# Earlier row splits, and one selection for the first two experts, in an encoder layer with a mixture of experts

## The reference

```python
h = (_layer_norm(x) * (1 + scale2) + shift2)                 # 512 rows of 1024
logit_g = h @ w_router_group + b                             # 4 groups, top 1
logit_e = h @ w_router_expert + b                            # 8 experts of that group, top 2
# each token goes to 2 of 32 experts, weighted with the softmax of its logits
y = (silu(xb @ w_exp_gate[e]) * (xb @ w_exp_up[e])) @ w_exp_down[e]
f = sum of the two weighted y of a token
x = LN(alpha * x + gate2 * f)
```

## Time and profile before

| | us |
|---|---|
| median of 3 runs | 959.95 |
| lowest, highest | 956.57, 960.58 |
| profiled execution | 959.74 |
| its span, first to last instruction | 958.10 |
| routing, first TensorE instruction behind the output projection | 430.74 |
| first product of expert 0 | 455.25 |

### The profile page before, as it was taken

The page is one execution under the profiler, slowest core; times in us unless marked ns, Lnnn a source line. Parts: engine busy times, 40 slices in busy tenths (PEclk is TensorE's granted clock), DMA queues, the critical chain, the costliest instruction groups (busy, mean ns, idle before and its releaser), DMA issues.

```text
span 958.1 us, 11740 instructions
## 1 busy us (share of the span) xinstructions
PE 908.5 (95%) x4381; PEld 547.7 (57%) x4381; DVE 375.9 (39%) x646; ACT 244.6 (26%) x357; POOL 113.6 (12%) x142
## 2 busy tenths in 40 slices
PE   3999999999999999999999999999998999998994
PEld 2567766888888888786454444444444444443331
DVE  4533443565344236798531232222221231322135
ACT  2422244432333225446411111101011110111024
POOL 2210366000001000000000000000000000000031
PEclk9999999999999999999999999999998999999997
DMA  9985654265565623809999999999999999999974
GB/s 370 348 282 175 253 218 177 89 230 208 200 240 147 183 91 114 278 0 401 384 404 400 410 427 425 427 424 429 429 426 424 375 395 427 426 426 427 423 290 136
DMA packets 47510, 295.53 MB, mean 308 GB/s; under 512 B 5046, under 2 KB 7190, under 8 KB 32082
## 3 DMA queue, kind: packets, MB, share of 16 engines
q1 hardware_dynamic: 37216, 263.99, 68.6%
q0 software_dynamic: 9616, 29.02, 9.0%
q10 hardware_dynamic: 610, 1.66, 0.5%
HBM read 275.81 MB, written 23.09 MB: 312 GB/s over the span
## 4 chain that ended last, share of the span: by engine, by line
PE 88%; DVE 3%; DMA 2%; issue 2%; SPq 2%; ACT 2%; POOL 0%; DVEq 0%; POOLq 0%; ACTq 0%
PE bank L627 85%; PE bank L929 2%; SPq L397 2%; DMA modraw<-in_w_mod 1%; DMA y_first<-round_y,pos_y 1%; PE bank L832 0%; PE bank L692 0%; DVE wo_lo L1766 0%; DMA round_y<-yout,store_row 0%; PE bank L911 0%; DVE y_second L2189 0%; DVE y_second L2202 0%; ACT w_hi L1181 0%; POOL y_second L615 0%; ACT sg_hid L1415 0%
## 5 line engine op out<-in xcount | busy, mean ns | idle before, releaser
L627 PE MATMUL bank<-down_w,hid_t 128*64 128x512 f32 x512 | 123.9, 627 | 8.1 <-issue 5.6
L627 PE MATMUL bank<-h_hi,w_hi 128*128 128x512 f32 x320 | 124.8, 390 | 0.3 <-ACT h_hi L1215 0.3
L627 PE MATMUL bank<-h_hi,w_lo 128*128 128x512 f32 x320 | 124.7, 390 | 0.0
L627 PE MATMUL bank<-h_lo,w_hi 128*128 128x512 f32 x320 | 124.6, 397 | 0.0
L627 PE MATMUL bank<-gate_w,x_by_pair 128*64 128x512 f32 x256 | 112.5, 592 | 0.8 <-ACT x_by_pair L1181 0.8
L627 PE MATMUL bank<-up_w,x_by_expert 128*64 128x512 f32 x256 | 112.6, 592 | 0.0
L627 PE MATMUL bank<-gate_w,x_by_expert 128*64 128x512 f32 x256 | 112.5, 592 | 0.0
L627 PE MATMUL bank<-up_w,x_by_pair 128*64 128x512 f32 x256 | 112.5, 592 | 0.0
L1415 ACT ACTIVATE sg_hid<-bank 64x512 f32<-64x512 f32 x33 | 19.5, 591 | 315.0 <-PE bank L627 315.0
L2047 DVE TENSOR_TENSOR sg_hid<-bank,sg_hid 64x512 f32<-64x512 f32 x32 | 22.2, 695 | 196.4 <-ACT sg_hid L1415 196.3
L1601 DVE TENSOR_TENSOR w_lo<-raw,w_hi 128x1024 fp32r<-128x1024 f32 x56 | 68.5, 1225 | 76.9 <-ACT w_hi L1181 76.8
(11 more groups left out here) (329 smaller groups left out, 1310.3 us busy)
## 6 DMA issues: line engine op xcount, KB each, us to landing
down_w<-in_w_exp_down SPq DMA_DIRECT2D x32, 2048.0 KB, 16.6
gate_w<-in_w_exp_gate SPq DMA_DIRECT2D x30, 2048.0 KB, 16.0
up_w<-in_w_exp_up SPq DMA_DIRECT2D x30, 2048.0 KB, 20.5
modraw<-in_w_mod SPq DMA_DIRECT2D x24, 1024.0 KB, 7.7
raw<-in_w_in SPq DMA_DIRECT2D x9, 2048.0 KB, 9.8
round_y<-zrow POOLq DMA_DIRECT2D x6, 2048.0 KB, 7.7
raw<-in_w_branch_b SPq DMA_DIRECT2D x2, 2048.0 KB, 9.5
raw<-in_w_branch_a SPq DMA_DIRECT2D x2, 2048.0 KB, 10.6
```

Of the source, the lines that this page charges most:

```text
L627: return pe.matmul(out, lhsT, rhs, start=start, stop=stop, skip_group_check=True)
```

## The change

- ScalarE makes the high parts during the routing: the first right behind the copy of tile 2, the other three behind the copy of tile 3.
- GpSimd, not VectorE, makes the low parts, each when its high part and the transposes of its tile are done.
- Experts 0 and 1 are selected together from the split rows: one `sel` operation on VectorE in place of two, 16 `float32r` products in place of 24 float32 ones. `selected_alone` goes.
- The columns of both experts are made in two halves of four chunks; `x_rows_b` is a second row buffer.
- `gate_up` of expert 1 runs right behind that of expert 0; the transposes of expert 0's hidden rows stand in its middle, and `down` of expert 0 comes after it. Expert 1 has a PSUM bank and a hidden buffer of its own (`sg_second`).
- The selection for experts 2 and 3 moves behind `down` of expert 0.
- SyncE loads expert 3's halves in four DMAs instead of eight, and issues expert 4's gate and up weights ahead of expert 2's down weights.
- ScalarE's scaling of `res` (128x4096) moves behind the first `Silu`.

```diff
+        x_rows_b = at("x_rows_b", [128, 512], f32, S0 + 3584)
...
+        sg_second = at("sg_second", [128, DE], f32, T0 + 34816)
...
-            for e in range(3, NEXP - 2):
...
+            done = sp.value_load(tab[0:1, 1, 1:2], min_val=0, max_val=16)
+            for half, freed, loaded in ((slice(0, KC // 2), gum_half, e_half), (slice(KC // 2, KC), m_sem["gum"], e_gu[0])):
+                sp.wait_ge(freed, 1)
+                sp.sem_inc(sp_go, 1)
+                sp.wait_ge(x_sem["gum"], done + 1)
+                sp.sem_inc(sp_go, 1)
+                for tile, w in ((gate_w[0], w_exp_gate), (up_w[0], w_exp_up)):
+                    sp.dma_start(tile[:, half, :], gate_src(w, 3)[:, half, :]).then_inc(loaded, 16)
+            next_gate_up(4, 1)
+            next_down(2, 0)
+            next_down(3, 1)
+            for e in range(5, NEXP - 2):
+                next_gate_up(e, e % 3)
                 next_down(e - 1, (e - 1) % 2)
...
+            for i in range(TILES):
+                pool.wait_ge(act_h2hi, i + 1)
+                pool.wait_ge(pe_rt, 2 * i + 2)
+                pool.tensor_tensor(h2_lo[i][:, :, :], h2[i][:, :, :], h2_hi[i][:, :, :].bitcast(f32), ALU.subtract).then_inc(pool_h2lo, 1)
...
-            def selected_alone(a, bank, chunks):
...
-            def selected(chosen, bank, c):
-
-                for i in range(TILES):
+            def selected(chosen, bank, c, tiles=range(TILES), parted_rows=None):
+                for i in tiles:
+                    if parted_rows is not None:
+                        pe.wait_ge(parted_rows, i + 1)
                     for piece in (h2_hi, h2_lo):
                         x = mm(bank[:, :], chosen[:, i, :, :].rearrange("p a s -> p (a s)"), piece[i][:, 4 * c:4 * c + 4, :].rearrange("p k n -> p (k n)"),
                                start=(i == 0 and piece is h2_hi), stop=(i == TILES - 1 and piece is h2_lo))
...
+            def first_columns(half):
+                pe.wait_ge(m_sem["xr"], half + 1)
+                x_transposes((x_rows, x_rows_b)[half], B[4 + half]).then_inc(m_sem["xtr"], 1)
...
+            def first_experts():
+                main_gate_up(0)
+                main_gate_up(1)
+                main_down(0)
+                pe.wait_ge(dve_rt, 2)
+                turns_in_place(0)
+                pe.wait_ge(m_sem["sl"], 2)
+                selected(sel, B[4], 0).then_inc(m_sem["xs"], 1)
+                selected(sel, B[0], 1).then_inc(m_sem["xs"], 1)
+                main_transposes(1)
+                pe.wait_ge(m_sem["xr"], 3)
+                x_transposes(x_rows, B[2]).then_inc(m_sem["xtr"], 1)
+                main_down(1)
+                turns_in_place(1)
...
-            for h in range(2):
-                selected_alone(0, B[2 + h], slice(2 * h, 2 * h + 2)).then_inc(m_sem["xs"], 1)
-            for h in range(2):
-                pe.wait_ge(m_sem["xr"], h + 1)
-                x_transposes(x_rows, B[4 - 2 * h], range(2 * h, 2 * h + 2)).then_inc(m_sem["xtr"], 1)
+            selected(sel, B[2], 0, parted_rows=pool_h2lo).then_inc(m_sem["xs"], 1)
+            selected(sel, B[3], 1, range(2))
+            pe.wait_ge(act_rt, 2 * TILES + 1)
+            first_columns(0)
+            selected(sel, B[3], 1, range(2, TILES)).then_inc(m_sem["xs"], 1)
             pe.sem_inc(x_sem["ym"], 1)
             pe.sem_inc(x_sem["gum"], 1)
-            for e in range(2):
-                first_experts(e)
+            first_experts()
...
+            def high_part(i):
+                act.wait_ge(act_h2, i + 1)
+                copy(h2_hi[i][:, :, :], h2[i][:, :, :]).then_inc(act_h2hi, 1)
+
             chunk_order(2)
+            act.wait_ge(pe_out, 2 * TILES)
+            high_part(0)
             h2_columns(3, 0, (B[4], B[5]))
             chunk_order(3)
+            for i in range(1, TILES):
+                high_part(i)
...
+            def columns_in(xt, bank):
+                return copy(xt, bank[:, :].rearrange("p (k c s) -> p c k s", k=4, c=2))
+
+            for half, rows in enumerate((x_rows, x_rows_b)):
+                act.wait_ge(m_sem["xs"], half + 1)
+                copy(rows[:, :], B[2 + half][:, :]).then_inc(m_sem["xr"], 1)
+                act.wait_ge(m_sem["xtr"], half + 1)
+                columns_in(x_by_expert[:, 0:2, 4 * half:4 * half + 4, :], B[4 + half]).then_inc(m_sem["xt"], 1)
 
             act.activation(fin[:, 4, 0:1], eps_col[:, :], ACT.Silu)
-            copy(res[:, :, :], res[:, :, :], scale=ALPHA).then_inc(act_res, 1)
...
+            def first_experts():
+                act.wait_ge(dve_rt, 2)
+                main_silu(0)
+                copy(res[:, :, :], res[:, :, :], scale=ALPHA).then_inc(act_res, 1)
+                hid_columns(m_sem, B[3], hid_t, 0)
+                main_silu(1)
+                turns_in_place(0)
+                act.wait_ge(m_sem["xs"], 3)
+                copy(x_rows[:, :], B[4][:, :]).then_inc(m_sem["xr"], 1)
+                hid_columns(m_sem, B[3], hid_t, 1)
+                act.wait_ge(m_sem["xs"], 4)
+                act.wait_ge(m_sem["xtr"], 3)
+                copy(x_rows[:, :], B[0][:, :]).then_inc(m_sem["xr"], 1)
+                turns_in_place(1)
...
-            for a in range(2):
-                chosen_rows(sel[:, :, a, :], a).then_inc(m_sem["sl"], 1)
+            chosen_pair(sel, slot_of[:, 0:2, :]).then_inc(m_sem["sl"], 1)
...
-                    dve.wait_ge(m_sem["xtr"], 3)
-                    columns_in(x_by_expert[:, 1, :, :].rearrange("p (c k) s -> p c k s", c=2), B[2]).then_inc(m_sem["xt"], 1)
-                    chosen_pair(sel, slot_of[:, 2:4, :]).then_inc(m_sem["sl"], 1)
-                    for i in range(TILES):
-                        dve.wait_ge(act_h2hi, i + 1)
-                        dve.tensor_tensor(h2_lo[i][:, :, :], h2[i][:, :, :], h2_hi[i][:, :, :].bitcast(f32), ALU.subtract).then_inc(dve_h2lo, 1)
-                    out_rows(e)
...
+            def first_experts():
+                dve.wait_ge(m_sem["xs"], 2)
+                chosen_pair(sel, slot_of[:, 2:4, :]).then_inc(m_sem["sl"], 1)
+                hidden(0)
+                dve.wait_ge(dve_rt, 2)
+                dve.wait_ge(act_rt, 2 * TILES + 1)
+                ch.sync()
+                sides(0)
+                gate_rows(0)
+                hidden(1)
+                out_rows(0)
+                turns_in_place(0)
...
+                dve.wait_ge(m_sem["htr"], 2)
+                chosen_group(4)
...
```

More of the change, by code:

```diff
@@ L891, in _ @@
             x.then_inc(pe_lg, 1)
-            def selected_alone(a, bank, chunks):
-                cols = slice(128 * chunks.start, 128 * chunks.stop)
-                for i in range(TILES):
-                    for c in range(2):
-                        piece = h2[i][:, 4 * c + chunks.start:4 * c + chunks.stop, :].rearrange("p k n -> p (k n)")
-                        x = mm(bank[CAP * c:CAP * c + CAP, cols], sel[:, i, a, :].bitcast(f32), piece, start=(i == 0), stop=(i == TILES - 1))
-                return x
-            def selected(chosen, bank, c):
-                for i in range(TILES):
+            def selected(chosen, bank, c, tiles=range(TILES), parted_rows=None):
+                for i in tiles:
+                    if parted_rows is not None:
+                        pe.wait_ge(parted_rows, i + 1)
                     for piece in (h2_hi, h2_lo):
@@ L912, in x_transposes, with gate_up @@
                 return x
-            def gate_up(xt, s, bank, sm, halves=None, order=range(KC), half_done=None):
-                for n, kc in enumerate(order):
-                    if halves is not None and n == KC // 2:
+            def gate_up(xt, s, bank, sm, halves=None, half_done=None, ahead_of=None):
+                for kc in range(KC):
+                    if ahead_of is not None and kc == ahead_of[0]:
+                        ahead_of[1]()
+                    if halves is not None and kc == KC // 2:
                         pe.wait_ge(*halves)
-                    mm(bank[0:CAP, :], xt(kc), gate_w[s][:, kc, :], start=(n == 0), stop=(n == KC - 1))
-                    x = mm(bank[CAP:128, :], xt(kc), up_w[s][:, kc, :], start=(n == 0), stop=(n == KC - 1))
-                    if half_done is not None and n == KC // 2 - 1:
+                    mm(bank[0:CAP, :], xt(kc), gate_w[s][:, kc, :], start=(kc == 0), stop=(kc == KC - 1))
+                    x = mm(bank[CAP:128, :], xt(kc), up_w[s][:, kc, :], start=(kc == 0), stop=(kc == KC - 1))
+                    if half_done is not None and kc == KC // 2 - 1:
                         x.then_inc(half_done, 1)
@@ L1467, in with_further, with turns_in_place @@
                 main_silu(e)
[L1469 to L1480 removed]
+            def turns_in_place(e):
                 more, first = turns_of(e)
@@ L2129, in first_experts @@
                         further_round(e, dve.snap(first + r))
+            def first_experts():
[10 more added lines that the diff above has]
+                turns_in_place(0)
```

(10 more changed lines are left out.)

115 lines of the change are left out of this document (25 added, 90 removed).

## The result

| | runs | median us | lowest, highest |
|---|---|---|---|
| before, measured beside it | 13 | 958.92 | 956.57, 961.23 |
| after | 13 | 963.76 | 961.63, 969.96 |

The ratio is 1.0058, interval 1.0042 to 1.0075: the changed kernel is 0.6% slower. The predicted 964.5 is 0.7 us off. The profiled execution took 964.45 us, with a span of 962.8.

A forecast was written before the change was run, and what follows sets the result against it. TensorE and the weight stream were taken to limit each other by turns, TensorE's progress through experts 0 to 5 deciding the end. -3.8 + 7.1 + 2.1 = +5.4; 959.74 + 5.4 - 0.6 = 964.5 us, range 955.3 to 967.5.

The forecast's parts named there:

- What bounds the kernel: From 440 us TensorE and the weight stream limit each other by turns; a TensorE delay at 450 us is passed on.
- TensorE's own work: Selections of experts 0 and 1: one block for two saves 3.6 us, copy waits -0.5, wider `sel` +0.3; sum -3.8 us.
- ScalarE, 0 to +0.1: During the routing: the four high parts fit between ScalarE's other work, at 0 to +0.1 us.
- GpSimd beside VectorE: Routing chain ahead of `sel`: three VectorE operations each wait for a whole GpSimd subtraction, +7.1 us, bounds 0 and 7.6.
- the second case: Routing chain: short VectorE operations slip through beside GpSimd, no delay or idle clock, 955.4 us; chance 0.2.
- The clock: First selection: TensorE stands idle about 7 us and then runs at a lower clock, +2.1 us, bounds 1.7 and 3.4.
- TensorE at expert 2: Start of expert 2 on TensorE: later by -3.8 + 7.1 + 2.1 = +5.4 us.
- From TensorE to the end: Weight loads from 462 us on: the shift stays, except that larger and reordered loads give -0.6 us, bounds 0 and -2.
- The border: End time: 964.75 us separates within 0.5% (chance 0.51) from slower by over 0.5% (chance 0.39).
- yield once: Routing chain: GpSimd's subtractions hold it only once, 2.4 us and 1.7 us of clock, 960.0 us; chance 0.1.
- the third case: Transfer queue near 462 us: it runs empty about 6 us and the delay grows, 966.5 to 969 us; chance 0.08.

The follow-up runs named there:

- plain delay: The kernel before with eleven fillers of 128x256 on TensorE right behind the wait for `sel`, nothing else changed: 964.30 us, +0.56%.
- the memsets: The changed kernel with two GpSimd memsets in place of each subtraction, the low parts left out of the selection: 958.01 us, -0.10%.
- two kernels with unused subtractions: The kernel before with four GpSimd subtractions whose result nothing uses, of 128x1024 (967.06 us, +0.8%) or of 128x512 (962.22 us, +0.35%).
- the run with seven fillers: The changed kernel with seven more TensorE fillers of 128x512 ahead of the wait for the first routing's counts: 962.44 us, +0.35% against the kernel before.
- the plain pair: The changed kernel with experts 0 and 1 selected together in plain float32, the split made behind it by ScalarE and VectorE: 959.21 us, +0.07%.
- the kernel with low parts on VectorE: The changed kernel with GpSimd subtracting only the first tile and VectorE the other three behind `sel`: 957.54 us in both runs, -0.10% and -0.18%.

## Why the prediction was right

- **What bounds the kernel.** Confirmed. The plain delay of 5.2 us came through as 5.5, and the stretch from 462 to 544 us was where the queue lost it.
- **TensorE's own work, -3.8.** Within its bounds, at -3.4, though not by a row of its own. By the memsets it is 2.8 us at expert 2, and they still have `sel` 0.5 us late and TensorE waiting 0.27 us more for it (0.56 against 0.29); that makes -3.6 for the products. In the kernel after, +4.7 less 6.6 for `sel`, 0.3 for that wait and 1.5 for the clock behind it leaves -3.7. The product term was 3.6 by itself, so the 0.5 us put down for the waits on ScalarE's copies are not seen; with the 0.3 for the wider `sel` the step is -3.4.
- **ScalarE, 0 to +0.1.** Right: its copy for the last tile stands at 441.25, before 441.23, and `gate_half` at 447.58 for 447.56.
- **GpSimd beside VectorE, +7.1.** Right, at 6.3 (`both` at 455.11 for 448.79). The 6.6 at `sel` hold 0.3 us of slower counting products, which belong to the clock. The step assumed that `lg` would be 0.4 us late; it was 0.1, and the chain got further before it was first held, since a reduce passes freely. Three gaps, three operations of 2.1 to 2.5 us. This was the disputed step, since no row of before showed a short operation held, and the second case (955.4) hung on it. The two kernels with unused subtractions show the cause by themselves.
- **The clock, +2.1.** Right, at 1.8: 1.5 us behind `sel`, by the run with seven fillers, and 0.3 on the counting products. The row it was sized by (5.35 us for 16 products behind 1.51 us of idle) was a matter of luck, since elsewhere an idle time as long costs nothing (last section).
- **TensorE at expert 2, +5.4.** It was +4.7: -3.4 + 6.3 + 1.8. The chain was 0.8 us less and the clock 0.3 less, and 0.4 less was saved.
- **From TensorE to the end, -0.6.** Not confirmed: +4.7 at expert 2 is +4.7 at the end. The reordered loads brought nothing, as in the plain pair. The two misses of 0.7 and 0.6 us cancel, so that 964.5 meets the profiled 964.45.
- **The border.** The kernel before, measured again, is 958.92 and not 959.95. The bound of 0.5% falls from 964.75 to 963.71, and 963.76 is just past it; the interval of the ratio (1.0042 to 1.0075) takes in both sides. I held "within 0.5%" for likelier (0.51) than "slower" (0.39); by the medians the slower side came true, by 0.05 us.
- **The other cases.** Short operations do not slip through, and the chain does not yield once: each subtraction found a gap. The queue did run empty, as the third case foresaw (expert 3's load was 8.7 us late, 23 GB/s from 462 to 467 us), but the delay did not grow by it: TensorE's first wait for weights is still at 655 us.

Not asked in the prediction is what the second case would have been worth. It gave 955.4 for the subtractions without the hold. The memsets are that case, and they took 958.0, against 958.3 for the kernel before beside it: of 2.8 us gained at expert 2 little arrives. For delays shift and time agree within 1.8 us; for gains of 2.4 to 2.8 us the medians fell 0.33 to 1.87 us. In the memset kernel a part is seen to go at one place:

```profile
709.91 6.32 PE L643 MATMUL bank<-down_w,hid_t 128*64 128x512 f32 x16 [3.23 <-issue]
727.09 0.76 PE L643 MATMUL bank<-h_hi,sel_x 128*128 128x512 f32 x1 [4.00 <-issue]
```

Before, the same block started at 711.99 behind 1.67 us of idle and took 5.35 us. Now it idles 3.23 and takes 6.32 us, and the further round behind it is only 1.35 us ahead of before (728.44). Executions of one kernel differ by 4.7 us (before) to 8.3 us (after) here, so how much of a gain of 2 to 3 us is lost on the average stays open.

## What to carry to other kernels

Work moved to an idle GpSimd is not free if it reads SBUF while VectorE runs a chain of short dependent operations with two SBUF inputs. Three subtractions of 2.3 us each cost the chain 6.3 us; with shorter instructions less of their length was lost (2.5 us by four of 1.27, 1.75 us by four copies of 1.0). So add up the GpSimd instructions that run beside the chain, not the chain's own. Put such work where VectorE is idle, or on VectorE itself behind the result that is waited for; one SBUF input on VectorE is no safe sign, since a `TENSOR_SCALAR` was held too. Ask what the engine behind the chain does meanwhile: TensorE's clock fell in the pause, and that was a fifth of what was lost (1.8 of 8.1 us). And here delays arrived whole at the end, while of gains only a part did (0.3 to 1.9 us of 2.4 to 2.8, 4.1 of 7.4); for the largest the transfer queue had nothing unused left, for the others the reason stays open.

## What the runs showed of the hardware

- A plain copy on GpSimd (1.0 us for 128x1024) takes less than half a subtraction (2.33), and holds VectorE too, for as long as it runs.
- Behind 2.27 us without work TensorE's next 3.67 us of products took 5.13. Behind 0.56 us the selection started without such a loss (four products in 1.20 us).
- The length of an idle time does not say alone whether TensorE loses clock behind it. Behind 1.31 us of idle, 16 products of the same shapes took 3.65 us in the plain pair and 5.35 in the kernel with low parts on VectorE, in this order:

```profile
665.09 3.65 PE L635 MATMUL bank<-down_w,hid_t 128*64 128x512 f32 x16 [1.31 <-issue]
```
```profile
709.95 5.35 PE L640 MATMUL bank<-down_w,hid_t 128*64 128x512 f32 x16 [1.31 <-issue]
```
